# Seven-product units: nine more, and the feed-forward's units moved between the two column blocks of their pair

## The reference

```python
gates = jax.nn.sigmoid(gate_logits.reshape(B, T, N_BRANCHES, D_MODEL) + b_branch_gates[l])   # ga*, gb*: h @ w_in
mixed = (gates[:, :, 0] * y_a + gates[:, :, 1] * y_b) @ w_out[l]                             # wo*
f = (jax.nn.silu(h @ w_ffn_gate[l]) * (h @ w_ffn_up[l])) @ w_ffn_down[l]                     # fg*, fu*, d**
y = jnp.concatenate([a_out, c_out, m_out], axis=-1) * jax.nn.silu(gate)
o = y @ w_o[l]                                                                               # o00.. o13
```

## Time and profile before

| | |
|---|---|
| median of 3 runs | 2280.22 us (2280.21 to 2281.05) |
| the profiled execution | 2281.4 us, span 2279.4 us, granted clock 0.999 |
| PE | 2267.1 us busy (99%), 10645 matmuls |
| PE weight load | 1897.2 us (83%) |
| DVE | 1648.4 us (72%), 2158 instructions |
| ACT | 1227.9 us (54%), 1599 instructions |
| POOL | 30.5 us (1%) |
| DMA | 458.34 MB, mean 201 GB/s |

### The profile page before, as it was taken

One profiled execution on the slowest core, in us unless ns is written; L12 is line 12 of the kernel. 1 busy time (PEld: TensorE's weight loads), 2 busy tenths in 40 slices (PEclk: granted clock), 3 DMA queues, 4 the chain that ended last, 5 costly groups with the idle time before them and its releaser, 6 DMA issues.

```text
span 2279.4 us, 27834 instructions
## 1 busy us (share of the span) xinstructions
PE 2267.1 (99%) x10645; PEld 1897.2 (83%) x10645; DVE 1648.4 (72%) x2158; ACT 1227.9 (54%) x1599; POOL 30.5 (1%) x40
## 2 busy tenths in 40 slices
PE   9999999999999999999999999999999999999998
PEld 7888888888888888888888888888888888888887
DVE  6677777756666668898888988875668756676864
ACT  6555655444445755555555555565655446556443
POOL 0000000000000000000000000000000000000000
PEclk9999999999999999999999999999999999999999
DMA  8666665766668557756665776766565665656654
GB/s 295 179 194 197 194 192 166 228 202 202 194 202 275 176 163 251 241 192 226 219 200 174 244 228 213 251 206 197 160 180 166 223 209 148 203 163 182 173 198 136
DMA packets 261604, 458.34 MB, mean 201 GB/s; under 512 B 23808, under 2 KB 63744, under 8 KB 260832
## 3 DMA queue, kind: packets, MB, share of 16 engines
q1 hardware_dynamic: 260192, 453.94, 63.8%
q0 software_dynamic: 848, 2.10, 0.6%
q10 hardware_dynamic: 432, 0.53, 0.1%
HBM read 437.09 MB, written 4.19 MB: 194 GB/s over the span
## 4 chain that ended last, share of the span: by engine, by line
PE 92%; DVE 5%; DMA 1%; ACT 1%; issue 1%; SPq 0%; DVEq 0%; ACTq 0%
PE pm L1120 27%; PE pm L1122 27%; PE pm L1121 27%; PE pb L762 1%; DVE wl L2509 1%; DVE wl L2523 1%; PE pb L1041 1%; PE pb L944 1%; PE pb L1042 1%; PE pb L1043 1%; DVE raw L2517 1%; PE pm L1042 1%; PE pm L1041 1%; PE pm L1043 1%; PE pb L842 1%
## 5 line engine op out<-in xcount | busy, mean ns | idle before, releaser
L2523 DVE TENSOR_TENSOR wl<-raw,wh 128x1024 fp32r<-128x1024 f32 (+2 forms) x722 | 866.2, 1208 | 500.0 <-ACT wh L1671 496.8
L1671 ACT ACTIVATE wh<-raw 128x1024 fp32r<-128x1024 f32 (+2 forms) x722 | 749.4, 1044 | 734.8 <-PE pm L1122 665.0
L1120 PE MATMUL pm<-wh,hTh 128*128 128x512 f32 x702 | 275.1, 392 | 0.8 <-DVE wl L2523 0.8
L1121 PE MATMUL pm<-wl,hTh 128*128 128x512 f32 x702 | 273.3, 389 | 0.0
L1122 PE MATMUL pm<-wh,hTl 128*128 128x512 f32 x702 | 273.3, 389 | 0.0
L1120 PE MATMUL pm<-wh,xT3h 128*128 128x512 f32 (+1 forms) x640 | 249.0, 389 | 0.0
L1122 PE MATMUL pm<-wh,xT3l 128*128 128x512 f32 (+1 forms) x640 | 244.6, 382 | 0.0
L1121 PE MATMUL pm<-wl,xT3h 128*128 128x512 f32 (+1 forms) x640 | 244.4, 382 | 0.0
L1120 PE MATMUL pm<-wh,x2Th 128*128 128x512 f32 x544 | 211.6, 389 | 0.0
L1121 PE MATMUL pm<-wl,x2Th 128*128 128x512 f32 x544 | 211.6, 389 | 0.0
L1122 PE MATMUL pm<-wh,x2Tl 128*128 128x512 f32 x544 | 211.6, 389 | 0.0
(11 more groups left out here) (512 smaller groups left out, 3760.8 us busy)
## 6 DMA issues: line engine op xcount, KB each, us to landing
raw<-in_w_in SPq DMA_DIRECT2D x286, 512.0 KB, 4.0
raw<-in_w_ffn_gate SPq DMA_DIRECT2D x88, 512.0 KB, 4.9
raw<-in_w_ffn_up SPq DMA_DIRECT2D x88, 512.0 KB, 5.7
raw<-in_w_ffn_down SPq DMA_DIRECT2D x88, 512.0 KB, 5.1
raw<-in_w_o SPq DMA_DIRECT2D x64, 512.0 KB, 4.3
raw<-in_w_in SPq DMA_DIRECT2D x68, 256.0 KB, 3.3
...
```

What stands on the lines that cost most here:

```text
L1120: e.matmul(o, ah[:, kk, t], h[:, c], start=first and half >= joined, stop=False)
L1121: e.matmul(o, ah[:, kk, t], l[:, c], start=False, stop=False)
L1671: e.activation(h[:, 0:n], r[:, 0:n], ACT.Copy).then_inc(s["hi"], 1)
L2523: e.tensor_tensor(l[:, 0:n], r[:, 0:n], h[:, 0:n].bitcast(F32), ALU.subtract).then_inc(s["lo"], 1)
```

## The change

Nine units are added: `gs1` to `gs3` (the two gate blocks `ga`, `gb` of c = 1 to 3), `ws0` and `ws2` (output projection of the first block), `fs0`, and `os00`, `os02`, `os10` (output projections of the two layers). All units of the feed-forward, and `ws0`, `os00`, `os10`, stand between the two groups of their pair (`middle`): the first group sums its last 12 slices first, the unit adds to it, and then comes the second group. The three gate units, `ws2` and `os02` stand in front as before. The activation's forms get buffers by place and activation (`shapes`), and four more are computed (hT, mixT, and yT in each layer). The results of `wo*` and `o**` are first added in SBUF (`joined`) and then squared and multiplied from there (`sums_squares`, `scaled`); before, they were read from PSUM. Constants that say at which step an operation is due get smaller. There are 1591 steps. The diff, cut to its core:

```diff
-PRODUCT, SQUARED, CARRIED, SPLIT, GATHERED, LATER = 9, 11, 14, 27, 7, 14
-KO = (12, 13, 14, 15, 0, 1, 2, 3, 4, 5, 8, 9, 10, 11, 6, 7)
+PRODUCT, SQUARED, CARRIED, SPLIT, GATHERED = 3, 5, 8, 22, 2
+KO = (12, 13, 14, 15, 0, 1, 2, 3, 4, 5, 6, 7, 8, 9, 10, 11)
+SHAPES = {"gs": 0, "ws": 1, "fs": 2, "ds": 3, "os": 6}
...
+    def pair(unit, act, names, blocks, ks=k16, middle=False):
+
+        ks = list(ks)
+        if middle:
+            add(names[0], act, blocks[0], 0, kts=ks[4:])
+        out.append(Group(unit, act, [(blocks[0], 512)], ks[:4], ev=None))
+        out[-1].pair, out[-1].joins, out[-1].middle = [[(w, 512)] for w in blocks], names, middle
+        if not middle:
+            add(names[0], act, blocks[0], 0, kts=ks[4:])
+        add(names[1], act, blocks[1], 0, kts=ks[4:])
 
     w_in = a["w_in"][0]
...
+        if c:
+            pair(f"gs{c}", "hT", (f"ga{c}", f"gb{c}"), [w_in[:, o + 512 * c:o + 512 * c + 512] for o in (7184, 9232)])
+        else:
+            add("ga0", "hT", w_in, 7184)
+            add("gb0", "hT", w_in, 9232)
...
-    for c in range(4):
-        add(f"wo{c}", "mixT", a["w_out"][0], 512 * c, ev=("a" if c == 3 else "d", 2))
+    for c in (0, 2):
+        pair(f"ws{c}", "mixT", (f"wo{c}", f"wo{c + 1}"), [a["w_out"][0][:, 512 * i:512 * i + 512] for i in (c, c + 1)],
+             middle=not c)
...
-    def seven(name, act, joins, blocks, forms):
-        out.append(Group(name, act, [(blocks[0], 512)], range(4), ev=None))
-        out[-1].pair, out[-1].joins, out[-1].forms = [[(w, 512)] for w in blocks], joins, forms
...
-            if c:
+            pair(f"fs{c}", "x2T", (f"fg{c}", f"fu{c}"), [w[:, 512 * c:512 * c + 512] for w in (w_g, w_u)], middle=True)
...
-        for c in range(4):
-            if part < 3 and c % 2 == 0:
-                seven(f"ds{part}{c}", f"fT{part % 2}", (f"d{part}{c}", f"d{part}{c + 1}"),
-                      [rows[:, 512 * i:512 * i + 512] for i in (c, c + 1)], part + 1)
-            add(f"d{part}{c}", f"fT{part % 2}", rows, 512 * c, kts=range(4 if part < 3 else 0, 4 * n), ev=("d", 2))
+        if part == 3:
+            for c in range(4):
+                add(f"d3{c}", "fT1", rows, 512 * c, kts=range(4 * n))
+            return
+        for c in (0, 2):
+            pair(f"ds{part}{c}", f"fT{part % 2}", (f"d{part}{c}", f"d{part}{c + 1}"),
...
+            if (l, c) < (1, 2):
+                pair(f"os{l}{c}", "yT", (f"o{l}{c}", f"o{l}{c + 1}"), [w_o[:, 512 * i:512 * i + 512] for i in (c, c + 1)],
+                     KO, middle=not c)
+            else:
+                add("o12", "yT", w_o, 1024, kts=KO)
+                add("o13", "yT", w_o, 1536, kts=KO)
...
-        if g.forms:
-            w.wait_ge(s["f_l"], 2 * PARTS[g.forms - 1][0] + 2)
+        for k in ks:
+            if g.act in ("fT0", "fT1"):
+                w.wait_ge(s["f_l"], 2 * PARTS[int(g.name[2])][0] + k // 2 + 1)
+            else:
+                sem, value = ready(p, g.act, k, int(g.name[2]) if g.act == "yT" else 0)
+                w.wait_ge(s[sem], value)
         for i, form in enumerate(FORMS):
             j = p.slab_at[n + i]
...
             if b:
                 free(b)
-                bank[b] = ("q_c", u) if b == 4 else ("q_d", 4 * u)
-                w.wait_ge(s["s_l"], g.forms + 1)
-            elif form != "t4":
-                w.wait_ge(s[f"ev_{before.ev[0]}"], p.evac[before.name] - (form == "b22"))
+                bank[b] = ("q_c", u) if b == 4 else ("q_d", p.gathers[g.name] + 4)
+                w.wait_ge(s["s_l"], p.shape(g.name) + 1)
+            elif form == "b22" or form == "b21" and not g.middle:
...
+        yield from forms(6 + l, O + 5)
         if l == 0:
-            yield p.end["o03"]
+            yield from memory_low(1, 0)
+            yield from memory_low(1, 1)
+        w.wait_ge(s["pv"], 12 * l + 12)
+        yield from gathered(f"os{l}0")
+        for half in range(2):
+            joined(f"os{l}0", 0, half)
+        if l == 0:
+            yield from memory_low(1, 2)
+        yield O + 26
+        scaled(m.WO2, f"o{l}0", m.BC3, loads)
+        if l == 0:
+            yield from memory_low(1, 3)
+        yield p.end[f"o{l}1"]
+        for half in range(2):
+            joined(f"os{l}0", 1, half)
+        yield p.end[f"o{l}1"] + 5
+        scaled(m.WO2, f"o{l}1", m.BC3, loads)
...
+        yield from forms(1, E + 8)
+        yield from gathered("ws0")
+        for half in range(2):
+            joined("ws0", 0, half)
+        yield E + 28
+        scaled(m.WO, "wo0", m.BC, 16)
+        yield p.end["wo1"]
+        for half in range(2):
+            joined("ws0", 1, half)
...
+                    yield from forms(2, p.first["fg0"] + 3)
+                yield from gathered(f"fs{c}")
+                yield p.done[f"fg{c}"]
+                for half in range(2):
+                    joined(f"fs{c}", 0, half)
+                if c in SHAPED:
+                    yield from forms(SHAPED.index(c) + 3, p.done[f"fg{c}"] + 4)
+                yield p.end[f"fu{c}"]
+                for half in range(2):
+                    joined(f"fs{c}", 1, half)
             if q:
```

More of the change, by code:

```diff
@@ L94, in __init__ @@
         self.n = sum(w for _, w in cols)
-        self.pair = self.joins = self.forms = None
+        self.pair = self.joins = None
+        self.middle = False
 def weight_groups(a):
@@ L234, in __init__ @@
                 self.end[g.name] = n
+                if g.middle:
+                    self.done[g.joins[0]] = n
                 continue
@@ L998, in background @@
         yield from mix_turns()
[L999 removed]
+        yield from row_sums(p.end["yb3"] + 58, m.msum, "mrd", 5, "mss", "mem")
         yield from mk_turns(0)
@@ L1028, in seven @@
             elif form == "t4":
-                out, lhs, b = A[:, 1, :], [[x[:, 2 + k, late] for k in range(2)] for x in act], None
+                out, lhs, b = A[:, 1, :], [[x[:, k, late] for k in ks[2:]] for x in act], None
             else:
@@ L1051, in tensor_program @@
     n = 0
-    firsts, seconds = ([g.joins[i] for g in p.groups if g.pair] for i in range(2))
+    opened = [g.joins[0] for g in p.groups if g.pair and g.middle]
+    firsts, seconds = ([g.joins[i] for g in p.groups if g.pair and (i or not g.middle)] for i in range(2))
     for g in p.groups:
@@ L1226, in out_squares @@
             squares(acc[:, half, :], m.ssq[key][:, half * 4 + c:half * 4 + c + 1])
-    def out_last(name, dst):
-        acc = m.pm[p.acc[name]]
-        for half in range(2):
-            e.activation(dst[:, half, part(3)], acc[:, half, :], ACT.Copy).then_inc(s["ev_a"], 1)
     def attention(l, r, which):
@@ L1583, in background @@
                                  ).then_inc(s["rp_a"], 1)
-        for c in range(2):
-            yield p.end[f"wo{c}"]
-            out_squares(f"wo{c}", "wo", c)
+        E = p.end["yb3"]
+        yield from forms_high(1, E + 11)
+        yield from first_taken("ws0")
+        yield E + 24
+        sums_squares("wo0", "wo", m.WO)
+        yield from first_taken("ws2")
+        yield p.end["wo1"] + 3
+        sums_squares("wo1", "wo", m.WO)
         for c in range(4):
-            yield 500 + 2 * c
+            yield E + 36 + 2 * c
             w.wait_ge(s["mm"], p.end["gb3"])
@@ L2391, in background @@
                 low_across(3)
+                yield from forms(0, p.end["v3"] + 58)
             for br in range(2):
```

329 lines of the change are left out of this document (188 added, 141 removed).

## The result

The changed kernel takes **2317.9 us** (median of 5 runs, 2316.24 to 2319.48) against 2280.62 (2280.21 to 2281.33, 5 runs); the ratio is 1.0162, 95% interval 1.0150 to 1.0174. The forecast was 2303 in a range of 2287 to 2312: slower, as said, but 37 us and not 22.

What follows compares the result with a forecast made beforehand. PE's own work was taken as the bound, with DVE able to hold it up. Added 36.8 us less saved 14.5 gave net 22.3 on 2281.4: 2303.7, or 2302.5 on the median's scale, stated as 2303, range 2287 to 2312.

Steps and rivals of the forecast that it cites:

- A unit bears 2.2 us of foreign work: In every unit: DVE's lead lets it do 2.2 us of work not the unit's own before PE must wait.
- Gate units, 12.9: `gs1` to `gs3`: evacuation, sum of branches, transposes and gather on DVE make PE 4.3 us late each, 12.9 added.
- `ws0`, 9.1: Start of `wo0`: 3.3 us waiting for `mixT`'s last slices, 5.7 for the forms' low part at b11, 0.1 of signal.
- `ws2`, 0.5: Second unit of the first output projection: 2.4 us of foreign DVE work against 2.2 borne, 0.5 added with signals.
- b11's low part can begin 3 x 2.72 - 1.39 = 6.8 ahead of b11: At each unit's start: with four split buffers, DVE begins b11's low part 6.8 us before PE needs it.
- `os00`, 7.6: First unit of `o00` to `o03`: forms 4.3 us late at b11, with the memory's low parts 7.6 late in all.
- `os02`, 2.4: Unit `os02`: products, joins and a memory piece, 4.0 us against 2.2 borne; 1.8 to 2.9 added, 2.4 taken.
- `os10`, 2.8: Start of the second layer's output projection: as `os00` without memory work, b11 2.8 us late.
- The four waits are gone: Inside units of the kernel before: four waits for DVE's low parts, 2.3 us together, were taken to vanish.
- the units of feed-forward show none: Feed-forward units: no waits except small ones in the first `ds` of a part, 0.5 us each.
- the clock falls in the pauses: Rival: PE runs at half rate behind the pauses before b11 of `ws0` and `os00`, losing 2.2 us twice; 2307; 10 in 100.
- The first two rivals: New units run without a wait, 2266, 8 in 100; or only the forms' waits bind, 2282, no change, 7 in 100.

Runs made afterwards that it cites:

- dose: Changed kernel with the first 1 to 4 low parts computed twice in feed-forward units that hold no foreign work; 2329.5 us, ratio 1.0210.
- gates_spread: Changed kernel with gate units between `ga` and `gb`, transposes 30 steps later and both parts of `mixT` 33 and 34 later; 2304.76 us, ratio 1.0102.
- gates_front: Changed kernel with transposes 30 steps later and `mixT`'s parts 33 and 34 later, gate units left in front of their pair; 2307.16 us, ratio 1.0115.
- gates_middle: Changed kernel with the three gate units placed between `ga` and `gb` instead of in front; 2315.90 us, ratio 1.0152.
- kept_busy: Changed kernel with extra matmuls on PE, on data already there, filling the pauses before the four long waits; 2316.89 us, ratio 1.0156.
- late_wait: Changed kernel with the units' wait for the forms' low part moved from b11 to t1, the first product that reads them; 2313.67 us, ratio 1.0143.
- split27: Changed kernel with one number changed: the feed-forward product's high and low parts asked for at 27 steps, not 22; 2310.51 us, ratio 1.0127.

## Why the prediction was right in sign and wrong in size

- **"A unit bears 2.2 us of foreign work": right.** `dose` gives 2.1 to 2.4.
- **Gate units, 12.9: right in mechanism, 1.5 under.** 14.4 (3 x (3.45 + 1.36)). The pauses are 4.0 and not 4.3 each; the starts behind them had no term. That the cause is foreign work in the unit is shown by `gates_spread` and `gates_front`.
- **`ws0`, 9.1, and `ws2`, 0.5: 15.6 in all.** The wait for the forms is right: b11 began at 26.8 against 26.3, whether PE stood before it or ran at half rate. Missing are 1.5 at half rate behind b11, for which the sum had no term, 3.1 in and behind `ws2`, and about 0.9 of starts behind pauses. **The step that failed at `ws2` is the lead**, "b11's low part can begin 3 x 2.72 - 1.39 = 6.8 ahead of b11". In the changed kernel 16 of the 25 units have it, 6.81 each time. At `ws2` it is 4.3: b11's low part began at 720.88 and PE's b11 at 725.15.

```profile
710.80 1.06 ACT L1733 ACTIVATE wh<-raw 128x1024 fp32r<-128x1024 f32 x1 [3.54 <-DMA raw<-in_w_out]
...
711.89 2.59 DVE L2642 TENSOR_TENSOR wl<-raw,wh 128x1024 fp32r<-128x1024 f32 x2 [3.15 <-ACT wh L1733]
...
717.10 1.29 DVE L1905 TENSOR_TENSOR WO<-WO,pm 128x512 f32<-128x512 f32 x2
...
720.88 1.23 DVE L2628 TENSOR_TENSOR wl<-raw,wh 128x1024 fp32r<-128x1024 f32 x1 [0.23 <-ACT wh L1728]
...
731.38 0.50 PE L1075 MATMUL pb<-wh,shape 128*128 128x512 f32 x1 [1.81 <-DVE wl L2628]
```

  ACT stood 3.5 us for a weight load, DVE behind it 3.2 for ACT's high part, and only then came the gather and the joins of `ws0`, 3.9 us. In every trace that has `ws2` these stand at the same place of DVE's queue, but the wait for the load differs, and the lead goes with it:

| | ACT waits for the load | lead at b11 of `ws2` | pauses in `ws2` |
|---|---|---|---|
| changed kernel | 3.54 | 4.27 | 2.54 |
| gates_middle | 2.46 | 5.22 | 1.75 |
| gates_spread | 1.80 | 5.89 | 1.08 |
| gates_front | 1.13 | 6.57 | 0.55 |
| kept_busy | 1.06 | 6.59 | 0.51 |

  The five others have 2.8 to 3.6, 4.3 to 4.9 and 2.0 to 2.5. With the lead back the unit costs the 0.5 that was forecast for it. No run changed the load alone, so that the load is the cause is read from the traces; what made it late (issued 34.4 behind the start of the stage and 5.6 on its way, in `kept_busy` 33.9 and 3.9) stays open. What `late_wait` shows is that 4.3 of the stage hung on a wait that b11 does not need.
- **`os00`, 7.6, and `os02`, 2.4: 11.9 measured, 10.0 forecast.** `os00` is right: b11 began 20.8 behind the start of `o00` against 20.6, and pauses of 5.7, 1.5 at half clock and the starts behind them make 7.6. The memory's work was rightly seen as its neck: moving the forms' wait, or keeping the clock up, gave nothing there. The 1.9 are `os02`'s, with pauses of 3.7. The same step failed: its lead is 4.6 and not 6.8 (1869.85 and 1874.42), in every trace that has the unit. What took it is not separated by any run.
- **`os10`, 2.8: 3.8.** b11 began at 19.3 against 19.1; the pause is 2.05, and the half clock behind it, 1.70, lay on the path.
- **"The four waits are gone", "the units of feed-forward show none": right for the gate and up units, wrong for the down units and the stage**, which was forecast 2.2 shorter and is 3.2 longer. The step that failed is the reading of the changed constants: I followed the product and the transpose to their new steps, and not ACT's demand for their result, 5 steps earlier behind transfers that SP issues. At `os00` I had asked what is queued behind a waiting ACT; in the feed-forward I had not. Here too the lead is what went: 3.0, 3.1 and 3.2 at `ds02`, `ds12` and `ds22` in place of 6.8. `split27` gives 7.4 us back by that one number. With it the move and `fs0` together are worth 4.3 us to the feed-forward (697.3 against 701.6).
- **The rival "the clock falls in the pauses", held at 1 in 10, came true** in kind: four falls, not two, each 1.5 to 1.7 in the records and not 2.2, of which about 3.2 in all lay on the path. The rule of the Trainium skill, TensorE: Matmul & The Clock Gate, section HAM oscillation, which I had cited beside it, agrees: idle gaps between bursts did bring half rate back, here four times. That the trace of before has no such pause had kept its chance low, and was no evidence either way.
- The first two rivals (no waits; only the forms bind) are refuted by the waits of L2628 and L2642.

The spans differ by 38.3, the forecast by 22.3. Of the 16.0 between them 5.4 are the feed-forward; 6.0 the projection of the first block (3.1 `ws2`, 1.5 the half clock behind b11, 0.5 b11 itself, 0.9 starts behind pauses); 1.9 `os02`; 1.0 `os10` (1.7 half clock, less 0.7 by which its pause was shorter); 1.5 the gates; 0.2 the rest of the kernel. The feed-forward, `ws2` and `os02` hold 10.4 of the 16, most of it where the lead was not the 6.8 that the forecast took at every unit.
